# RWKV scan on one Trainium2 core: narrow products with a common stationary operand joined into wide ones

## What is computed

```python
def step(S, inp):
    r_t, w_t, k_t, v_t, kk_t, b_t = inp
    sa = einsum('bhij,bhj->bhi', S, -kk_t)
    S = S * w_t[:, :, None, :] + sa[..., None] * b_t[:, :, None, :] + v_t[..., None] * k_t[:, :, None, :]
    return S, einsum('bhij,bhj->bhi', S, r_t)
```

## Time and profile before

| | us |
|---|---|
| median of 3 runs | 3156.16 (3152.55 to 3157.61) |
| the profiled execution's own time | 3154.85 |
| its span, first to last instruction | 3153.0 |
| the scan in it | about 1411.6 to 1722.6 |
| mean granted TensorE clock | 0.979 |

### The profile page before, as it was taken

One profiled execution on the slowest core, in us unless ns is written; L12 is line 12 of the kernel. 1 busy time (PEld: TensorE's weight loads), 2 busy tenths in 40 slices (PEclk: granted clock), 3 DMA queues, 4 the chain that ended last, 5 costly groups with the idle time before them and its releaser, 6 DMA issues.

```text
span 3153.0 us, 49105 instructions
## 1 busy us (share of the span) xinstructions
PE 3022.5 (96%) x20814; PEld 2417.6 (77%) x20814; DVE 1030.0 (33%) x1482; ACT 945.4 (30%) x1080; POOL 1262.4 (40%) x443
## 2 busy tenths in 40 slices
PE   8999999999999967899999999998999999999998
PEld 6768778887888854769998788886888867678886
DVE  4441242223211147324444421126211145441213
ACT  3243322223222227432332322223222235432222
POOL 4354334443434341323331444444434346534433
PEclk9999999999999988999999999999999999999999
DMA  4202222222222222341111222222222221112222
GB/s 180 90 30 92 92 87 97 95 96 80 93 94 94 93 80 94 120 145 40 44 44 40 81 93 93 94 93 81 93 94 93 93 84 41 67 67 94 93 94 80
DMA packets 42572, 271.82 MB, mean 86 GB/s; under 512 B 4737, under 2 KB 4865, under 8 KB 12705
## 3 DMA queue, kind: packets, MB, share of 16 engines
q1 hardware_dynamic: 39312, 252.64, 22.6%
q10 hardware_dynamic: 3088, 16.65, 1.3%
HBM read 254.59 MB, written 14.68 MB: 85 GB/s over the span
## 4 chain that ended last, share of the span: by engine, by line
issue 58%; PE 22%; POOL 17%; DVE 3%; DVEq 0%; POOLq 0%; ACT 0%
POOL w_lo L487 15%; PE ps L793 8%; PE ps L619 3%; PE ps L620 3%; PE ps L621 3%; POOL ybuf L560 1%; PE ps L706 1%; PE ps L746 1%; PE ps L683 1%; POOL x_res L587 1%; DVE work L1442 0%; PE ps L778 0%; PE ps L765 0%; PE ps L713 0%; DVE work L1525 0%
## 5 line engine op out<-in xcount | busy, mean ns | idle before, releaser
L487 POOL TENSOR_TENSOR w_lo<-w_raw,w_hi 128x2048 fp32r<-128x2048 f32 x220 | 1023.9, 4655 | 1557.5 <-ACT w_hi L1034 1548.6
L619 PE MATMUL ps<-act_hi,w_hi 128*128 128x512 f32 x2240 | 894.8, 399 | 42.3 <-DVE act_lo L1470 23.3
L620 PE MATMUL ps<-act_lo,w_hi 128*128 128x512 f32 x2240 | 888.7, 397 | 0.0
L621 PE MATMUL ps<-act_hi,w_lo 128*128 128x512 f32 x2240 | 888.2, 397 | 0.0
L1034 ACT CAST w_hi<-w_raw 128x2048 fp32r<-128x2048 f32 x219 | 417.4, 1906 | 1040.9 <-PE ps L621 1016.6
L619 PEld LDWEIGHTS ps<-act_hi,w_hi 128*128 128x128 f32 x2240 | 424.3, 189 | 155.8 <-issue 26.3
L621 PEld LDWEIGHTS ps<-act_hi,w_lo 128*128 128x128 f32 x2240 | 424.3, 189 | 100.9
L620 PEld LDWEIGHTS ps<-act_lo,w_hi 128*128 128x128 f32 x2240 | 424.6, 190 | 100.5 <-issue 1.7
L619 PE MATMUL ps<-hid_hi,w_hi 128*128 128x512 f32 x1184 | 470.5, 397 | 10.7 <-POOL w_lo L487 8.4
L621 PE MATMUL ps<-hid_hi,w_lo 128*128 128x512 f32 x1184 | 467.8, 395 | 0.0
L620 PE MATMUL ps<-hid_lo,w_hi 128*128 128x512 f32 x1120 | 442.8, 395 | 0.0
(11 more groups left out here) (252 smaller groups left out, 2400.7 us busy)
## 6 DMA issues: line engine op xcount, KB each, us to landing
w_raw<-stream SPq DMA_DIRECT2D x224, 1024.0 KB, 4.8
spill<-work ACTq DMA_DIRECT2D x5, 2048.0 KB, 7.0
scratch<-spill SPq DMA_DIRECT2D x24, 256.0 KB, 3.8
work<-bias_in SPq DMA_DIRECT2D x1, 3072.0 KB, 18.9
work<-spill SPq DMA_DIRECT2D x12, 256.0 KB, 3.2
x_res<-x_in SPq DMA_DIRECT2D x2, 1024.0 KB, 8.1
spill<-area ACTq DMA_DIRECT2D x4, 512.0 KB, 3.4
area<-spill SPq DMA_DIRECT2D x7, 256.0 KB, 2.8
```

What stands on the lines that cost most here:

```text
L487: tt(w_lo[:, s, :], w_raw[:, s, :], w_hi[:, s, :].bitcast(F32), ALU.subtract).then_inc(S["lo_made"], 1)
L619: mm(out, wh, hi[:, k, :], start=(k == 0) if begin is None else begin, stop=False)
L620: mm(out, wh, lo[:, k, :], start=False, stop=False)
L621: return mm(out, wl, hi[:, k, :], start=False, stop=end)
```

## The change

Products that share a stationary operand become one product with a wider moving operand. The operands' places in SBUF change so that the moving ones lie side by side.

- K0 and K1 (chunks 0 to 3 and 4 to 7): K against R, KK and dg side by side, 192 columns, giving RkT, KakT and kT. b0 and b1: b against the same three, giving RbT, KabT and bT. A job of four chunks takes two PSUM banks with two chunks of 192 columns each. VectorE masks its two parts in halves of 256 columns and then ScalarE copies the third, waiting for VectorE's second part.
- WU: XT against KKT and Kv, 128 columns, giving W and U, both copied by ScalarE. MQ: W against bT and RbT, giving M and Q, both by VectorE. Each takes two neighbouring banks.
- The kinds in CROSSED write to the other head's partitions (rows 0 to 63 give partitions 64 to 127 and the other way round). The chunk matrices then lie crossed, and C, Yo and MQ cross back.
- ROUND and LAST are rewritten. scan(m+1) comes after LT0, decays(m+1) after LY1; the splits of tiles 1 to 4 come after vT, LX2, bonus and LY3. Banks are chosen as those that have rested longest, two neighbours for a wide job.
- A facility for issuing two jobs in alternation (in_turn, rwkv_steps) is added but its table TURNS is empty: each job is issued in one piece.

```diff
-        BY_TILE = {"R": 16, "KK": 17, "b": 18, "K": 19, "rk": 20, "dg": 21}
+        BY_TILE = {"R": 16, "KK": 17, "dg": 18, "b": 19, "K": 20, "rk": 21}
...
+        def rw_side_by_side(name, m, count):
+
+            at = {"R": BY_TILE["R"] + 8 * (m % 2), "KKT": SHARED["KKT"], "bT": 8 + 2 * (m % 2)}[name]
+            return area[:, at:at + count, :]
...
+        ROUND = [("WU", -1), ("KKT", 0), ("gs", -2), ("LY0", 0), ("gq", -2), ("MQ", -1), ("LX0", 0), ("C", -1), ("LT0", 0), ("S1", -1),
+                 ("LY1", 0), ("Yo", -1), ("gr", -2), ("S2", -1), ("K0", 0), ("LX1", 0), ("S3", -1), ("K1", 0), ("LT1", 0), ("gx", -2),
+                 ("S4", -1), ("LY2", 0), ("vT", 0), ("spread", 1), ("S5", -1), ("LX2", 0), ("LT2", 0), ("bonus", 0), ("S6", -1), ("LY3", 0),
+                 ("Kv", 0), ("LX3", 0), ("LT3", 0), ("LY4", 0), ("b0", 1), ("y", -1), ("sq", -1), ("LT4", 0), ("b1", 1), ("X", 1)]
+        STEPS_OF = {"y": 7, "K0": 4, "K1": 4, "b0": 4, "b1": 4}
+        RESULTS = {"WU": ("W", "U"), "MQ": ("M", "Q"), "K0": ("KakT0", "RkT0", "kT0"), "K1": ("KakT1", "RkT1", "kT1"),
+                   "b0": ("KabT0", "RbT0", "bT0"), "b1": ("KabT1", "RbT1", "bT1")}
+        CROSSED = ("kT", "bT", "vT", "KKT", "KabT", "X", "KakT", "RkT", "RbT", "MQ", "C", "Yo", "K0", "K1", "b0", "b1")
...
-        SPLIT_AFTER = {"kT": 1, "LT1": 2, "RbT": 3, "KKT": 4, "LT3": 0}
+        SPLIT_AFTER = {"vT": 1, "LX2": 2, "bonus": 3, "LY3": 4, "LT3": 0}
...
-                BANK[job] = turn % 7
...
+            wide = 2 if job[0] in RESULTS else 1
+            b = min(range(free_from, 8 - wide), key=lambda b: (max(used[b:b + wide]), b))
...
-            def by_head(out, lhs, rhs, start=True, stop=True):
+            WIDE = {"WU": ("XT", "KKT", 2), "MQ": ("W", "bT", 2), "K0": ("K", "R", 3), "K1": ("K", "R", 3), "b0": ("b", "R", 3), "b1": ("b", "R", 3)}
+
+            def by_head(out, lhs, rhs, start=True, stop=True, crossed=False):
                 for a in (0, 64):
                     b = a + 64
-                    inst = mm(out[a:b], lhs[a:b], rhs[a:b], start=start, stop=stop)
+                    inst = mm(out[64 - a:128 - a] if crossed else out[a:b], lhs[a:b], rhs[a:b], start=start, stop=stop)
                 return inst
...
+                if kind in WIDE:
+                    name, beside, count = WIDE[kind]
+                    width = 64 * count
+                    per_bank = 512 // width
+                    first = 4 if kind in ("K1", "b1") else 0
+                    for n in range(STEPS_OF.get(kind, NCH)):
+                        at = BANK[kind, m] + n // per_bank, width * (n % per_bank)
+                        rhs = rw_side_by_side(beside, m, count)[:, :, 64 * (first + n):64 * (first + n) + 64]
+                        yield by_head(ps[:, at[0], at[1]:at[1] + width], chunk(rw(name, m), first + n), rhs, crossed=kind in CROSSED)
+                    return
...
-                    if kind == "LX0" and m + 1 < NT:
+                    if kind == "LY1" and m + 1 < NT:
                         decays(m + 1)
...
+                        elif kind in RESULTS:
+                            act.wait_ge(S["dve_jobs"], OUT[results_of(kind)[1], m][1])
+                            inst = nc.scalar.copy(half_tile(part, m), wide_result(part, kind, m))
...
+                    if kind in RESULTS:
+                        for part in results_of(kind):
+                            if part in BY_ACT:
+                                continue
+                            p = wide_result(part, kind, m)
+                            if part[:4] == "KabT":
+                                tt(half_tile("XT" + part[-1], m), p, mask4("firstT"), ALU.mult)
+                            inst = tt(half_tile(part, m), p, mask4("strict" if part[0] == "K" else "incl"), ALU.mult)
+                            if part == "KabT1":
+                                dve.drain()
+                                inst = tt(chunks(rw("XT", m)), chunks(rw("XT", m)), mask("eye"), ALU.add)
+                            inst.then_inc(S["dve_jobs"], 1)
+                        continue
...
-                    if kind == "LY0" and m + 1 < NT:
+                    if kind == "LT0" and m + 1 < NT:
                         scan(m + 1)
```

More of the change, by code:

```diff
@@ L375, in build @@
         NO_JOB = ("sq", "gq", "gr", "scale", "split", "out", "outa", "outb")
-        BY_ACT = ("kT", "bT", "vT", "KKT", "Kv", "W", "U", "C", "Yo")
-        NEEDS = {"W": ("LT4", "KKT"), "U": ("LT4", "Kv"), "M": ("W", "bT"), "C": ("U", "kT", "vT", "bT"), "Q": ("W", "RbT"), "gs": ("y",),
-                 "Yo": ("U", "vT", "RkT", "RbT"), "Kv": ("KakT", "vT"), "S1": ("M", "C"), "y": ("S6", "Q"), "LY0": ("KabT", "X")}
+        BY_ACT = ("kT0", "kT1", "bT0", "bT1", "vT", "KKT", "Kv", "W", "U", "C", "Yo")
+        NEEDS = {"WU": ("LT4", "KKT", "Kv"), "MQ": ("W", "bT1", "RbT1"), "C": ("U", "kT1", "vT", "bT1"), "gs": ("y",),
+                 "Yo": ("U", "vT", "RkT1", "RbT1"), "Kv": ("KakT1", "vT"), "S1": ("M", "C"), "y": ("S6", "Q"), "LY0": ("KabT1", "X")}
         for n in range(2, 7):
@@ L399, in build @@
             jobs += 1
-            JOB[job], OUT[job] = jobs, (engine, counts[engine])
+            for part in results_of(job[0]):
+                engine = "act_jobs" if part in BY_ACT else "dve_jobs"
+                counts[engine] += 1
+                OUT[part, job[1]] = (engine, counts[engine])
             if job[0][0] == "S" or job[0] == "gs":
                 continue
-            if last_turn:
-                BANK[job] = 2 + turn % 5 if job[0] != "gx" else 4 + job[1] % 2
-            else:
-                BANK[job] = turn % 7
@@ L407, in build @@
[L407 to L410, removed]
-        LAST_IN_BANK = dict(in_bank)
+            wide = 2 if job[0] in RESULTS else 1
+            b = min(range(free_from, 8 - wide), key=lambda b: (max(used[b:b + wide]), b))
+            BANK[job] = b
+            BANKS_BEFORE[job] = [in_bank[a] for a in range(b, b + wide) if a in in_bank]
+            for a in range(b, b + wide):
+                used[a], in_bank[a] = jobs, job
@@ L862, in made, with ready @@
                         seen[name] = count
[L863 to L867 removed]
+                def ready(kind, m):
                     if kind == "gs":
@@ L882, in rwkv_pe, with in_turn @@
                         made(*OUT[need, m])
-                    if (kind, m) in BANK_BEFORE:
-                        made(*OUT[BANK_BEFORE[kind, m]])
+                    for last, tile in BANKS_BEFORE.get((kind, m), ()):
+                        for part in results_of(last):
+                            made(*OUT[part, tile])
                     waited()
+                def in_turn(first, second, alone, ones, twos):
+                    ready(*first)
+                    if not alone:
+                        ready(*second)
+                    one, two = rwkv_steps(*first), rwkv_steps(*second)
+                    left, others = STEPS_OF.get(first[0], NCH), STEPS_OF.get(second[0], NCH)
+                    for n in range(alone):
+                        next(one)
+                        left -= 1
+                    if alone:
+                        ready(*second)
+                    while left + others:
+                        for n in range(min(ones, left)):
+                            inst = next(one)
+                            left -= 1
+                            if not left:
+                                inst.then_inc(S["job_mm"], 1)
+                        for n in range(min(twos, others)):
+                            inst = next(two)
+                            others -= 1
+                            if not others:
+                                inst.then_inc(S["job_mm"], 1)
+                todo = ORDER[begin:end]
+                for n, (kind, m) in enumerate(todo):
+                    if kind[:3] == "out":
+                        output_step(kind, m)
+                    if kind in NO_JOB or n and (todo[n - 1], todo[n]) in TURNS:
+                        continue
+                    if n + 1 < len(todo) and (todo[n], todo[n + 1]) in TURNS:
+                        in_turn(todo[n], todo[n + 1], *TURNS[todo[n], todo[n + 1]])
+                        continue
+                    ready(kind, m)
                     rwkv_job(kind, m).then_inc(S["job_mm"], 1)
```

144 lines of the change are left out of this document (82 added, 62 removed), and 4 rows, old and new, of the table ROUND.

## The result

The changed kernel takes 3132.03 us (median of 4 runs, 3130.69 to 3137.33), the kernel before 3156.89 beside it (4 runs, 3152.55 to 3161.81). The ratio is 0.9924, with a 95% interval of 0.9905 to 0.9943. Forecast were 3153.0 with a range of 3144.5 to 3162.0: the gain is 25 us, not 3. The profiled execution took 3132.39 us with a span of 3130.6, which is 22.4 us less than the span before.

What follows compares the result with a forecast made beforehand. TensorE's own time was taken to bound the middle tiles. Terms: -5.0 (wide products) - 1.2 (first tile) + 2.4 + 0.7 (last tile) = -3.1 us, giving 3153 us against the 3156.16 median; range 3144.5 to 3162.

Steps and rivals of the forecast that it cites:

- What bounds the kernel: Middle tiles of the RWKV scan: only TensorE's own time counts, never idle in a 36.02 us tile.
- The products with a common operand: Scan tiles: wide products replace ten narrow jobs, 0.6 us less a tile, 5.0 us in eight.
- The crossing: Joints between straight and crossed jobs: cost from 0 to 0.15 us each; taken as 0.
- The first tile: First scan tile: idle before LY0 falls from 3.4 to 2.2 us, gaining 1.2 us; lower clock stays.
- The last tile: Last scan tile: split held beside w_lo, LX3 5.0 us late, losing 2.4 us; LT4 to WU costs 0.7.
- the clock falls in the last tile: Rival: last tile's hole of up to 5.0 us lowers the clock, 3.0 us more, 3156; chance 0.14.
- the joints cost: Rival: 123 straight-crossed meetings at 0.10 to 0.15 us add 12.3 to 18.5, 3165 to 3171.5; chance 0.12.
- the wide products bring nothing: Rival: wide instructions take 88 and 58 to 62 ns, giving 3158 to 3160.4 us; chance 0.09.
- the last tile does not stall: Rival: splits get in between GpSimd's instructions, 2.6 us gained instead of 2.4 lost, 3148; chance 0.12.

Runs made afterwards that it cites:

- (6): Changed kernel with CROSSED empty and GpSimd's w_lo of the last tile in four pieces of 512 columns: 3147.96 us, ratio 0.9965.
- (5): Changed kernel with GpSimd's w_lo of the last tile in four pieces of 512 columns instead of one of 2048: 3127.48 us, ratio 0.9900.
- (1): The straight kernel: changed kernel with CROSSED empty, so every product writes its own head's partitions; wide products kept: 3157.30 us, ratio 0.9993.
- (2): Kernel before (narrow products, old order) with crossing alone, the same results crossed: 3161.42 us, ratio 1.0004.
- (7): Changed kernel with five pairs a tile issued in alternation and the last tile's w_lo in four pieces: 3122.23 us, ratio 0.9879.
- (12): As (7), with two more pairs issued in alternation, K0 with LX1 and K1 with LT1: 3129.55 us, ratio 0.9900.
- (4): Changed kernel with five pairs a tile of a straight and a crossed job issued in alternation: 3124.48 us, ratio 0.9889.
- (11): Changed kernel with X moved ahead of b1, so that straight WU stands behind crossed b1: 3132.12 us, ratio 0.9920.
- 3: Changed kernel with b0 moved behind LT4, next to b1, leaving fewer joints of straight and crossed jobs: 3133.27 us, ratio 0.9909.
- 9: Changed kernel with only the wide jobs K0, K1, b0, b1 and MQ crossed (another output, same work): 3131.57 us, ratio 0.9909.
- 10: Changed kernel with only the narrow jobs vT, KKT, X, C and Yo crossed (another output, same work): 3147.52 us, ratio 0.9961.
- (8): Kernel before with crossing alone, plus the last tile's w_lo in four pieces: 3156.06 us, ratio 0.9984.

## Why the prediction was wrong, step by step

**What bounds the kernel: right.** TensorE's own time sets the middle tiles; with VectorE at 17.4 us, where 18.3 were forecast, no bank or mask came late.

**The products with a common operand: right.** Forecast were 0.6 us a tile from 82 and 54 ns an instruction; the straight kernel shows 0.58 (36.02 to 35.44), and 81 ns (1.30 us for 16) and 55 (1.75 for 32). Eight tiles at 0.6 are 4.8 us; the prediction's sum has 5.0, which changes nothing.

**The crossing: the step that failed.** The prediction reads: "What may cost is a joint between the two kinds: from 0 (jobs already touch, so less can't be) to the 0.15 us". The reason that excluded a gain was false. By the runs, jobs touch in the earlier trace rows because the second needs the same two quarters of the array as the first, and so each instruction waits its turn (29 ns); a job on the other two quarters does not, and the two together start every 14.4 ns. Whether it is the load or the product that waits was not separated. The term was to be 0 to +18.5 us. It was 3.94 us a tile the other way in an undisturbed tile, and 20 to 25 us in the kernel: 20.5 between (6) and (5), and 25.2 between the medians of (1) and of the changed kernel, which were not measured side by side (by their ratios it is 21.8). The steps towards it, in the order in which they could have been seen: the straight pair itself overlaps, since "two halves run together"; the same sentence of the prediction says why, and stops at the pair. The question to ask was what a third instruction would share with the two in flight. The Trainium skill has it in the very list that the prediction cites, "TensorEngine Tiling (Array Packing)", section Key Properties: the first item says that a change of mode drains TensorE, the second that different tiles can execute loads and products in parallel. I took the first and passed over the second. The traces agree with it: starts come every 29 ns in a straight job and every 14.4 ns where a straight and a crossed job alternate.

**Why the two parts need each other.** Behind a narrow job a joint gives 0.1 to 0.2 us, behind a wide one mostly 0.4 to 0.6. The wide instructions made the joints worth having. Crossed narrow jobs alone (2) had 8.4 us less in flight over the six tiles; 5.2 of it came back as idle time there, and the last tile took the rest. How far the second job may run ahead, a count of instructions or a time, was not measured by itself; that wide jobs give more fits a count.

**The first tile: right in size, by compensation.** Forecast -1.2 us, measured -1.3 up to spread 1. LY0 started 6.2 us behind b0, not 6.7: the masks by hand were 0.5 us too long. But the lower clock lasted 10.2 us instead of 6.8, some 1.7 us lost, and the straight kernel (1), which shares both, took 21.6 us up to spread 1, as before. So the 1.3 us must come from the joints; the 1.2 us of the forecast went into the clock.

**The last tile: right in the waits, not in the clock.** One split beside w_lo took 4.54 us, LX3 came 4.20 us late for 5.0 forecast, and LT4 to WU cost 0.61 for 0.7. What the Trainium skill says in "SBUF — State Buffer", section Who interferes with whom, that such a VectorE instruction and such a GpSimd instruction shut each other out, agrees with this row and with the pieces of (5). The rival "the clock falls in the last tile" happened too, at a price of 6.8 us (half of 13.7) instead of 3.0. In the sum it is hidden: +1.9 us where the forecast had +3.1. Without crossing (1) the same part grew by 8.3 us, with 20.5 us of lower clock. Of the 6.4 us between the two, 3.4 are clock (half of 6.8), and the rest I put down to the joints.

**The rivals.** That the joints cost, that the wide products bring nothing, and that the last tile does not stall are all refuted by rows above. None of the rivals was a gain from crossing, which is why the range ended at 3144.5.

**What is left open.** TensorE's idle time grows as the instructions go faster: over the six tiles 0.0 us in (1), 3.7 in the changed kernel, 8.2 in (7), 12.4 in (12). Nearly all of it (in 12 all but 1.3 us) is put down to the issue, but that name covers two things. In (7) 2.4 us of the 8.2 and in (12) 3.5 of the 12.4 lie ahead of the first instruction of a job, some of them 0.10 us behind the end of the copy that the job needs, as at S1 in (4). The rest lies inside jobs, behind no semaphore, and the long ones at the same instruction of the program in each kernel: behind the sixth of KKT of tile 3, TensorE stands for 0.66 us in the changed kernel, 1.42 in (7) and 1.15 in (12), and behind the thirtieth of KKT of tile 6 for 0.60, 0.93 and 1.21. That speaks for the place in the instruction stream. Packets of 16 KB on the queue that loads instructions come 43 times in these tiles in each of the four kernels, and most pauses begin within 3.5 us of one; but such stretches cover three quarters of the time anyway, so that this is no proof. In the changed kernel the four pauses over 0.5 us begin 1.3 to 1.8 us behind a packet that came 5.3 to 6.3 us after the last one, where the median is 4.1; four other packets came as late, and behind three of them no pause follows. Whether TensorE's instructions arrive too late was not tried by an experiment of its own.

## What to carry to other kernels

Before saying that an edge costs nothing because two blocks of work already touch, name the resource on which they touch, and ask whether the change moves one of them off it. Where TensorE works in quarters, let neighbouring jobs use different ones, and put a wide job, not a narrow one, ahead of the change; issuing two such jobs in turn takes more than the joint does, until the issue or the clock takes it back. A gain that only one tile (11) or only the pairs themselves (12) show is not a gain of the kernel: measure the whole.

## What was not expected of the hardware

- Matrix products on different quarters start out of program order: b1's first two at 1505.18 ahead of LT4's last six at 1505.21. An instruction of 32 to 64 columns starts every 29 ns among its like and every 14.4 ns in turn with the other kind.
- In the kernel before, with holes of 1.27, 0.73 and 0.62 us in the last tile, the clock stayed up there. It fell there in every other kernel with one w_lo: with a hole of 3.96 to 4.21 us in the changed one, 1, 3, 4, 9, 10 and 11, for 13.7 us (20.5 in 1 and 10), and with holes of 1.74 and 2.29 us in (2), for 13.7. With the pieces it did not fall there in (5) and (6), with holes ahead of LX3 of 1.11 and 0.86 us, but did for 10.2 us in (7), with 1.11, and in (8) and (12). So the long hole is not the only cause.
- Short falls also came inside full tiles: in (1), from 1503.1 us on, the clock was low for 6.8 us in a tile whose 38.56 us had no idle time at all.

```profile
1499.90:1538.46 38.56, 38.56 (x917) 35.48 (x913) 17.64 (x42) 12.39 (x21) 12.12 (x10) 0.91 0.14 44
```
